# FF1 block 0 in two parts, with its down products issued in block 1 and tiles 1 to 4 normed by a different split of engines

## What is computed

```python
def trunk_layer(x, mod, lp, k_ctx=None, v_ctx=None):
    sh1, sc1, g1, sh2, sc2, g2, sh3, sc3, g3 = mod      # silu(cond) @ w_ada + b_ada, nine parts
    h = modulate(rms_norm(x, lp['g_ff1']), sh1, sc1)    # h * (1 + scale) + shift
    x = x + 0.5 * g1 * swiglu(h, lp['w_ff1_in'], lp['w_ff1_out'])
    h = modulate(rms_norm(x, lp['g_mix']), sh2, sc2)
    ...
    x = x + g2 * (merged @ lp['w_out'])
    h = modulate(rms_norm(x, lp['g_ff2']), sh3, sc3)
    x = x + 0.5 * g3 * swiglu(h, lp['w_ff2_in'], lp['w_ff2_out'])

def swiglu(h, w_gu, w_dn):
    a, u = jnp.split(h @ w_gu, 2, axis=-1)
    return (jax.nn.silu(a) * u) @ w_dn
```

## Time and profile before

| what | us |
|---|---|
| median of 3 runs | 1688.76 (1687.05 to 1701.29) |
| the profiled execution | 1701.97 |
| its span on core 3, the slowest, which the page shows | 1700.4 |
| spans of cores 0 to 7 | 1685.8, 1686.3, 1699.9, 1700.4, 1686.5, 1686.1, 1680.7, 1681.4 |

### The profile page before, as it was taken

How to read it: one execution, slowest core, us unless ns; L and a number is a source line. 1 busy time by engine, 2 the same in 40 slices (tenths; PEclk the granted TensorE clock), 3 DMA queues, 4 the chain that set the end, 5 groups by cost and what they waited for, 6 DMA issues and landing times.

```text
span 1700.4 us, 25281 instructions; the slowest of 8 cores (1680.7 to 1700.4 us)
## 1 busy us (share of the span) xinstructions
PE 1536.0 (90%) x8548; PEld 695.4 (41%) x8548; DVE 956.5 (56%) x1646; ACT 494.2 (29%) x739; POOL 158.2 (9%) x235
## 2 busy tenths in 40 slices
PE   1689999999999995698889888999999999999998
PEld 1234444444444442243434444444334444444443
DVE  2256556555566554464546665345366666666666
ACT  2651110111111125745636566235421111111110
POOL 2131000000000012300000000021210000000000
PEclk9799999999999997787889899999999999999999
DMA  9906442345432332457225355584322222222005
GB/s 183 243 1 91 75 67 37 48 74 76 75 48 43 59 87 99 101 116 142 37 56 120 99 113 113 138 186 75 50 38 38 37 38 38 38 38 38 13 1 198
DMA packets 35788, 134.68 MB, mean 79 GB/s; under 512 B 5072, under 2 KB 5200, under 8 KB 33616
## 3 DMA queue, kind: packets, MB, share of 16 engines
q0 software_dynamic: 22560, 79.88, 30.3%
q1 hardware_dynamic: 13104, 53.18, 9.3%
HBM read 191.95 MB, written 20.97 MB: 125 GB/s over the span
## 4 chain that ended last, share of the span: by engine, by line
PE 79%; DVE 6%; issue 5%; ACT 4%; DMA 4%; POOL 1%; DVEq 0%; ACTq 0%; SPq 0%; POOLq 0%
PE ps L413 76%; ACT arena L422 3%; DVE arena L430 3%; PE ps L410 3%; DMA arena<-wts 3%; DVE arena L426 2%; POOL arena L603 1%; DMA arena<-xin 1%; DVE arena L436 1%; ACT L422 1%; DVEq L183 0%; DVE arena L445 0%; DVE arena L442 0%; ACTq L183 0%; POOL arena L323 0%
## 5 line engine op out<-in xcount | busy, mean ns | idle before, releaser
L413 PE MATMUL ps<-arena 128*128 128x512 bf16 (+3 forms) x7108 | 1476.7, 363 | 132.9 <-DVE arena L430 53.5
L413 PEld LDWEIGHTS ps<-arena 128*128 128x128 bf16 x7108 | 646.7, 100 | 919.6 <-issue 336.8
L430 DVE SCALAR_TENSOR_TENSOR arena<-ps,arena 128x512 f32<-128x512 f32 (+2 forms) x860 | 562.5, 714 | 89.6 <-ACT arena L422 47.1
L422 ACT ACTIVATE arena<-ps 128x512 f32<-128x512 f32 (+4 forms) x418 | 266.1, 652 | 1045.8 <-PE ps L413 526.7
L426 DVE TENSOR_TENSOR arena<-arena,ps 128x512 bf16<-128x512 f32 (+1 forms) x198 | 130.2, 658 | 411.7 <-PE ps L413 382.4
L426 DVE TENSOR_TENSOR arena<-arena 128x512 f32<-128x512 f32 (+10 forms) x196 | 141.6, 738 | 114.9 <-ACT arena L422 89.3
L323 POOL DMA_DIRECT2D arena<-wts x150 | 79.9, 536 | 1255.5 <-PE ps L413 1025.0
L422 ACT ACTIVATE arena<-arena 128x512 bf16<-128x512 f32 (+6 forms) x230 | 165.6, 748 | 86.9 <-DVE arena L426 25.0
L410 PE MATMUL ps<-arena 128*128 128x65 bf16 (+3 forms) x1440 | 80.6, 214 | 25.5 <-DVE arena L436 16.0
L603 POOL TENSOR_TENSOR arena<-arena 128x512 bf16<-128x512 f32 (+3 forms) x77 | 75.9, 1010 | 186.4 <-ACT arena L422 99.3
L410 PEld LDWEIGHTS ps<-arena 64*128 64x128 bf16 (+1 forms) x1440 | 53.5, 98 | 79.0 <-issue 69.8
(11 more groups left out here) (12 smaller groups left out, 6.1 us busy)
## 6 DMA issues: line engine op xcount, KB each, us to landing
arena<-wts POOLq DMA_DIRECT2D x150, 512.0 KB, 8.8
arena<-xin SPq DMA_DIRECT2D x8, 1024.0 KB, 13.6
xspill<-arena SPq DMA_DIRECT2D x4, 2048.0 KB, 7.0
arena<-xspill SPq DMA_DIRECT2D x4, 2048.0 KB, 14.7
yoT<-arena SPq DMA_DIRECT2D x32, 256.0 KB, 2.3
arena<-ebias SPq DMA_DIRECT2D x12, 640.0 KB, 5.1
arena<-ebias SPq DMA_DIRECT2D x8, 768.0 KB, 5.4
nkT<-arena SPq DMA_DIRECT2D x8, 256.0 KB, 2.9
```

The lines of the kernel that those rows point to most:

```text
L413: return P.emit("pe", lambda e: e.matmul(out, lhsT=lhsT, rhs=rhs, start=start, stop=stop), reads=reads, writes=writes, inc=inc)
L422: return P.emit("act", lambda e: e.activation(out=out, in_=in_, func=func, **kw), reads=reads, writes=writes)
L430: return P.emit("dve", lambda e: e.scalar_tensor_tensor(out=out, in0=in0, scalar=scalar, in1=in1, op0=op0, op1=op1), reads=reads, writes=w ...
```

## The change

It takes a buffer `HB5` of five slots for the silu(gate)*up of block 0, one for each tile. In block 0 only gate and up products are made, for all tiles; squares of tile t+2 and the norm of tile t+1 are emitted between the two pairs of tile t. The first squares of tile 1 are emitted before part "b" of tile 0. Squares of tiles 1 to 4 and the modulations are spread over other engines. Then the gate and up weights are released, the hook's adaLN matmuls follow, and block 1 issues the down products of block 0 ("owed") just ahead of those that it had, chunk by chunk. Block 0's down weights (unit 14) are released at the end of block 1. Token loads are held until earlier weight units.

```diff
+        HB5 = mem(oG + 16384, 10240, BF16, "p (t j n) -> p t j n", t=5, j=2)
+        P.claim(oG + 16384, 10240, [("hb5", t, j) for t in range(5) for j in range(2)])
...
+        def hbuf(hs):
+            return (HB, "hb", hs) if hs < 2 else (HB5, "hb5", hs - 2)
...
-                for ti, u in ((1, 6), (2, 10), (3, 13), (4, 15)):
+                for ti, u in ((1, 7), (2, 9), (3, 10), (4, 11)):
                     lazy_load(ti, after=wtok[u])
+                norm_tile(nidx, tiles[1], part="a", sq="apv")
                 norm_tile(nidx, tiles[0], part="b", mo="av", stat=stat0, mid=lambda: first_mod(acc))
...
-                if not first:
-                    ud, Dn, rd = wacq(("ffd", which, bi))
+                if first:
+                    for t in range(ntt):
+                        ff_GU(G, U, rg, ru, nj, tiles[t], 2 + t, jjs=[0])
+                        if t + 2 < ntt:
+                            norm_tile(nidx, tiles[t + 2], part="a", sq="pppapppa")
+                        if t + 1 < ntt:
+                            norm_tile(nidx, tiles[t + 1], part="b", mo="av")
+                        ff_GU(G, U, rg, ru, nj, tiles[t], 2 + t, jjs=[1])
+                    wrel(ug)
+                    wrel(uu)
+                    blk0_hook()
+                    owed = wacq(("ffd", which, bi))
+                    after_block(bi)
+                    continue
+                ud, Dn, rd = wacq(("ffd", which, bi))
...
-                        if first and step + 1 < ntt:
-                            norm_tile(nidx, tiles[step + 1], sq="a" if step == 0 else "pppppppa",
-                                      sc="vvvp" if step else "v")
-                        if first and step == 1:
-                            blk0_hook()
-                            ud, Dn, rd = wacq(("ffd", which, bi))
                     for m in range(8):
                         if m == 4 and step < ntt:
                             ff_GU(G, U, rg, ru, nj, tiles[step], step % 2, jjs=range(1, nj))
                             pump(2)
+                        if owed is not None and step < ntt:
+                            ff_DN(owed[1], owed[2], nj, tiles[step], 2 + step, ig, ms=[m])
                         if step >= 1:
                             ff_DN(Dn, rd, nj, tiles[step - 1], (step - 1) % 2, ig, ms=[m],
                                   chunk_done=chunk_done if last else None)
...
                 wrel(ud)
+                if owed is not None:
+                    wrel(owed[0])
+                    owed = None
```

More of the change, by code:

```diff
@@ L690, in build_program @@
         silc = [0]
+        def hbuf(hs):
+            return (HB, "hb", hs) if hs < 2 else (HB5, "hb5", hs - 2)
         def ff_GU(G, U, rg, ru, nj, tile, hs, jjs=None):
+            hb, hkey, hi = hbuf(hs)
             t0, n, cond = tile
@@ L705, in ff_GU @@
                 actv(SIL[:, ss, 0:n], bank_ap(ba)[:, 0:n], AF.Silu, [banks[ba]], [P.R("sil", ss)])
-                vtt(HB[:, hs, jj, 0:n], SIL[:, ss, 0:n], bank_ap(bu)[:, 0:n], ALU.mult,
-                    [P.R("sil", ss), banks[bu]], [P.R("hb", hs, jj)])
+                vtt(hb[:, hi, jj, 0:n], SIL[:, ss, 0:n], bank_ap(bu)[:, 0:n], ALU.mult,
+                    [P.R("sil", ss), banks[bu]], [P.R(hkey, hi, jj)])
         def ff_DN(Dn, rd, nj, tile, hs, ig, ms=range(8), chunk_done=None):
             t0, n, cond = tile
+            hb, hkey, hi = hbuf(hs)
             for m in ms:
@@ L713, in ff_DN @@
                 for jj in range(nj):
-                    mm(bank_ap(by)[:, 0:n], Dn[:, jj, m * 128:(m + 1) * 128], HB[:, hs, jj, 0:n],
-                       jj == 0, jj == nj - 1, [rd, P.R("hb", hs, jj)], [banks[by]], inc=(jj == nj - 1))
+                    mm(bank_ap(by)[:, 0:n], Dn[:, jj, m * 128:(m + 1) * 128], hb[:, hi, jj, 0:n],
+                       jj == 0, jj == nj - 1, [rd, P.R(hkey, hi, jj)], [banks[by]], inc=(jj == nj - 1))
                 vstt(xview(m, t0, n), bank_ap(by)[:, 0:n], DER[:, ig, m, cond:cond + 1], xview(m, t0, n),
```

## The result

The kernel after the change takes 1724.12 us (median of 4 runs, 1722.61 to 1724.81), against 1688.76 for the kernel before: 35.4 us more. The ratio, which is that of the means, is 1.0186, 95% interval 1.0128 to 1.0245: 31 us slower, between 22 and 41. The two differ because one of the three runs before took 1701.29. In some executions, of whichever kernel, the cores of one die show a lower granted clock and the time is some per cent longer; they are left out of all times and ratios. I forecast 1714 us, slower by over 1%. The side is right and the time lies in the range; it is at the dear end of it.

The account below looks back on a forecast made before the run. DMA waits bound the head, engine handovers the stretch after 85 us, PE that after 190 us. Block 0 +3.9, down products +15.6 and waits +6 sum to +25.5: 1714 us, range 1697 to 1727.

Parts of the forecast that it names:

- Part 1: Head of block 0: tile 1's squares stand ahead of tile 0's norm; first gate matmul at 65.4 instead of 42.90 us.
- Rival (c): Order not as read in block 0: tile 0 gated at 42 as before, 22 us come back, about 1692; chance 0.02.
- Rival (b): Head: x loads win the DMA engines from the weights, tile 1 lands before 48; -0.6, 1688 us; chance 0.08.
- Part 2: Block 0, cycle per tile from table load to table load: 16.2 us (14.3 to 17.9), three cycles 47.4.
- rival (a): Block 0 chain warm and undisturbed: cycles of 14.3, no collision, stalls of 3; +9, 1698 us; chance 0.24.
- Part 3: Block 0: GpSimd squares collide with VectorE; 6 us, for tile 3's squares alone, bounds 0 and 12.7.
- Part 4: End of block 0: 16.4 us from tile 4's table load to block 1's first up product, at 144.4; block 0 +3.9.
- Part 5: Block 1: 72 down matmuls moved there cost 15.6 us in full, plus 6 for waits (bounds 0 and 8).
- The sum: Whole kernel: +3.9 + 15.6 + 6 = +25.5 us, between +6 and +40, giving 1714 us on the median.

Follow-up runs that it names:

- the three repairs: Kernel after, with tile 1's squares behind tile 0's norm, no squares on GpSimd, and one eviction for owed and own down products: 1704.5 us.

## Why the prediction was right, and where it fell short

None of the three signs of being wrong came: the gate of tile 0 started at 69.33 (not before 50), block 1's first multiply was at 152.15 (not before 130), and block 1 took 67.0 to 67.9 us from there (not under 62).

**Part 1, the late gate: right in kind, 3.9 short.** First gate matmul 69.33 on core 0, forecast 65.4. The landing was 0.8 later than I had it. The rest is VectorE beside GpSimd: the scalings took 7.43 for 4.9 (2.5), the first modulations 0.6 more. The failed step is a sentence of this part: "The x loads themselves hardly move in time". As a stream that holds: tile 4's halves landed 26.0 and 26.9 us after their issues at 57.5 and 57.9, at 84 to 85, forecast 84. Within the stream it doesn't: tile 2's halves were there at 61.8 and 67.8, with the old loads at 66.8 and 72.7, and so its squares met tile 0's scalings and modulations. The old loads put the gate at 64.89 and gave 4.1 us back.

**Rival (c) had a wrong price.** "Then 22 us come back" took the stall for its cost. Ungated, tile 0 brought 9.6, because tile 1 lands only at 57.2 and its Ln then waits for tile 2's landing. To end a stall at the head of a chain brings only what the next link is not late by on its own.

**Rival (b)** fell by its own sign: tile 1's second half landed at 55.9, not before 48.

**Part 2, the cycle: right.** First scalings at 100.74, 117.44 and 133.03 are 16.7 and 15.6 apart, for 16.2 and 15.0. Counted by table loads, from tile 1's to tile 4's, the three cycles came to 52.9, forecast 47.4 + 6 = 53.4:

```profile
77.77 1.28 ACT L422 ACT_TABLE_LOAD   x1 [1.63 <-PE ps L413]
...
130.65 1.28 ACT L422 ACT_TABLE_LOAD   x1 [3.39 <-PE ps L413]
```

That the two are so near is partly luck: the squares cost 3.9 of the 6, and the cycles were 1.5 longer in all. The clock behaved as I took it, half low, half full:

```profile
94.00:96.00 2.00, 1.94 (x6) 0.57 0.05 12
96.00:98.00 2.00, 2.00 (x11) 1.00 0.00 0
```

At the end of tile 1's modulation PE was granted 0.57, and 1.00 in the next two microseconds; these windows answer to the earlier trace rows. So rival (a), the warm chain, fell on both of its conditions.

**Part 3, squares beside VectorE: the place right, the reach too small.** The mis-sized term is "I take 6". I took 6, "tile 3's alone, because only they overlap fully". Tile 1's chunks lost 3.9 (11.7 for 7.8), a cycle of 20.2 us; tile 0's scalings and modulations lost 4.7 more, which I had at nothing. 8.6 on the rows, 3.7 net against squares on ScalarE. The Trainium skill (SBUF — State Buffer, "Who interferes with whom") has a VectorE instruction with two SBUF inputs and a reading GpSimd one exclude each other. The runs agree: scaling pairs of 1.29 took up to 2.97 beside squares, and each was 1.29 without them. By that rule I had worked out 12.7, every overlapping square blocking in full; the rows give 8.6.

**Part 4, the end of block 0: 2.3 short.** From tile 4's table load (130.65) to block 1's first up product (149.37) 18.7 us, for 16.4. The request for unit 16 was at 142.78, 12.1 behind the table load instead of 10.2, and it took 6.4. Of the 1.9 more, 0.8 are the chunks of 256 columns, 5.2 for 4.4 (133.03 to 138.19): a modulation took 0.41, not the half of 0.48 that I estimated. PE then waited 2.26 with DMA as releaser, where I had it closely covered. That wait isn't the same on each core, nor is the clock behind it:

```profile
150.00:156.00 6.00, 6.00 (x29) 1.00 1.04 160
```

```profile
150.00:156.00 6.00, 4.77 (x15) 0.72 1.05 159
```

The first is core 4, which had waited 1.84 and kept the full clock; the second is core 5, which had waited 3.33 and didn't. The eight cores part in the same way: cores 1, 2, 4 and 6 waited 0.87 to 1.88, were granted 1.00 in this window and reached the yardstick at 215.7 to 217.3; cores 0, 3, 5 and 7 waited 2.26 to 3.94, were granted 0.72 to 0.77 and reached it at 219.8 to 221.9. Not all of that is the clock: between cores 4 and 5 it is 5.5, of which 3.8 lay already between their first up products (147.43 and 151.23). On core 0 PE was granted 0.58 from 150 to 152 us and 0.56 in the next two, so its first multiply came 2.8 behind its first up product and not 1.9, and the next multiply 6.1 behind that where cores 1, 2, 4 and 6 have 5.2. That is 1.8 which no part had.

**Part 5, block 1: right.** +21.3 on six cores, +22.2 on core 0 with its low clock, for 21.6. The half-steps of 7.62 (178.66 to 186.29) are 0.71 above the 6.9 they take with one eviction, where I had 0.7 for each group of eight.

**The sum.** On the profiled cores +32.0 for +25.5: 2.7 from Parts 1 to 3 together (tile 4's table load at 130.65 for 128), 2.3 from Part 4, 1.8 from the clock at block 1's start, less 0.3 from Part 5. By the median of the cores it is +30.6. What is not a matter of size is "what was done in block 0 in the shadow of waits is now paid": of the 21.3, the down products cost 13.1 in block 0, too. It didn't touch the sum, which went by the whole times of the blocks. But it says what the change gained: those 13.1, which the late gate, GpSimd and the slower tile cycle used up, so that block 1 still began 9.8 later.

What stays open: what remains between the three repairs and the kernel before at the yardstick (10.9 us) holds the down products, 15.6 of PE in a full block, and a wait for unit 16 (2.94 on core 1), less what the change gained in block 0; I have not separated these. The wait for unit 22 comes on top, behind the yardstick.

## What to carry to other kernels

Work moved out of a stage with waits is paid in full in a stage without, and only the part that really lay in a wait was free before: measure that part (here some 40%) before you move it. In in-order queues, nothing of a tile that has not landed may stand ahead of the work of one that has. Before you change which engine does an operation, look at what that operation holds back on its queue, and at what runs beside it: two scalings on GpSimd were worth some 6 us as a gate for fourteen squares.

## What the runs showed of the hardware

- VectorE and GpSimd, both reading SBUF, slow each other: a pair of scalings of 128x512 float32 takes 1.29 alone and up to 2.97, a tensor_scalar 0.48 to 0.55 alone and about 1.0, a GpSimd square 1.0 alone and up to 1.5. Eight chunks of a tile go from 7.8 to 14 us.
- Issuing the token loads of tiles 2 to 4 earlier didn't give the tokens more of the DMA engines in all, but changed which half tile came when: from issue to landing the eight halves of tiles 1 to 4 took 11.6 to 28.5 us (line 557 of the kernel after, below). The Trainium skill (DMA: Bandwidth & Descriptors, "Queues, rings and completion order") has each engine taking turns between queues; that tile 4 landed at 84 to 85 as forecast, and at 84.4 in the kernel before, agrees with it.

```profile
DMA to landing us min/median/max: 11.6/22.0/28.5
```

- ScalarE beside VectorE costs VectorE nothing that the rows show: its modulations run between 102 and 108 us beside the scalings of tile 2, and each pair of those took 1.29 (100.74). With the squares on ScalarE, which run before the scalings, a pair is 1.29, too (79.49).
- The cores of one run parted at one wait: four had waited 0.87 to 1.88 us ahead of block 1 and show a granted clock of 1.00 from 150 to 156 us, the four that had waited 2.26 to 3.94 show 0.72 to 0.77, and they came out of that block up to 6 us apart, some 2 of them by the clock.
